# Half blocks of the expert weights ahead of chunks 1 to 5 of a round instead of 2 to 7, and a gain buffer of two rows instead of four

## The reference

```
qh = hb @ w_q                          # 8 heads, two halves each
v1, i1 = top_k(qh1 @ keys1, 16);  v2, i2 = top_k(qh2 @ keys2, 16)
best, pos = top_k(v1 + v2, 16)         # of 256 pairs
eidx = i1 * 128 + i2;  gates = softmax(best)
act = gelu(hb . u_tab[eidx])
out = sum over heads and choices of gates * act * v_tab[eidx]
```

## Time and profile before

| | |
|---|---|
| median of 3 runs | 3056.21 us (3046.61 to 3059.09) |
| profiled execution | 3059.14 us, its span 3057.4 us |
| mean granted TensorE clock | 0.941 |
| PE busy | 2788.9 us, 91% |
| PE weight loads busy | 2321.6 us, 76% |
| DVE busy | 1881.6 us, 62% |
| POOL busy | 1296.4 us, 42% |
| ACT busy | 1040.0 us, 34% |
| DMA | 528.80 MB, mean 173 GB/s |

### The profile page before, as it was taken

One profiled execution on the slowest core, in us unless ns is written; L12 is line 12 of the kernel. 1 busy time (PEld: TensorE's weight loads), 2 busy tenths in 40 slices (PEclk: granted clock), 3 DMA queues, 4 the chain that ended last, 5 costly groups with the idle time before them and its releaser, 6 DMA issues. The chain is left out here.

```text
span 3057.4 us, 38838 instructions
## 1 busy us (share of the span) xinstructions
PE 2788.9 (91%) x14085; PEld 2321.6 (76%) x14085; DVE 1881.6 (62%) x3137; ACT 1040.0 (34%) x1640; POOL 1296.4 (42%) x618
## 2 busy tenths in 40 slices
PE   7998996787999998969989899999999959999996
PEld 5887874634777887857878689998999957888885
DVE  5443224376164445348345448777999959888887
ACT  4222221154223222323012223334556524444442
POOL 3443444000433443424124346775222237777773
PEclk9999998589999999989789899999999989999998
DMA  5443322000323443313001235556999989999993
GB/s 173 142 146 110 103 89 103 1 1 17 94 83 131 137 151 120 106 55 111 20 14 36 74 106 163 169 157 230 361 351 345 338 292 350 381 381 379 382 378 138
DMA packets 186247, 528.80 MB, mean 173 GB/s; under 512 B 13984, under 2 KB 96288, under 8 KB 166432
## 3 DMA queue, kind: packets, MB, share of 16 engines
q1 hardware_dynamic: 79776, 292.66, 29.4%
q0 software_dynamic: 18432, 134.23, 11.1%
q10 hardware_dynamic: 87936, 100.68, 9.7%
HBM read 475.08 MB, written 52.43 MB: 173 GB/s over the span
## 5 line engine op out<-in xcount | busy, mean ns | idle before, releaser
L345 POOL TENSOR_TENSOR ring_low<-ring,ring_high 128x1024 fp32r<-128x1024 f32 x323 | 790.5, 2448 | 1172.9 <-ACT ring_high L312 1172.9
L396 PE MATMUL ps<-u_high,ring_high 128*128 128x512 f32 (+1 forms) x1824 | 700.8, 384 | 42.7 <-DVE u_low L617 17.7
L397 PE MATMUL ps<-u_low,ring_high 128*128 128x512 f32 (+1 forms) x1824 | 693.3, 380 | 0.0
L398 PE MATMUL ps<-u_high,ring_low 128*128 128x512 f32 (+1 forms) x1824 | 690.2, 378 | 0.0
L312 ACT ACTIVATE ring_high<-ring 128x1024 fp32r<-128x1024 f32 x355 | 375.2, 1057 | 717.3 <-PE ps L398 538.5
L396 PEld LDWEIGHTS ps<-u_high,ring_high 128*128 128x128 f32 x1824 | 346.8, 190 | 113.2 <-issue 40.7
L398 PEld LDWEIGHTS ps<-u_high,ring_low 128*128 128x128 f32 x1824 | 346.8, 190 | 57.6
L397 PEld LDWEIGHTS ps<-u_low,ring_high 128*128 128x128 f32 x1824 | 347.3, 190 | 52.9 <-issue 1.3
L2303 POOL DMA_INDIRECT fetched_rows<-in_peer_uv,fetch_index x128 | 166.2, 1298 | 310.4 <-DVE ps L2323 271.6
L345 POOL TENSOR_TENSOR ring_low_more<-ring,ring_high_more 128x1024 fp32r<-128x1024 f32 x96 | 245.9, 2565 | 88.4 <-ACT ring_high_more L312 87.4
L2869 DVE TENSOR_TENSOR expert_product<-group_acts,group_weights 128x384 f32<-128x384 f32 x128 | 172.1, 1345 | 70.9 <-issue 44.1
(11 more groups left out here) (429 smaller groups left out, 4834.3 us busy)
## 6 DMA issues: line engine op xcount, KB each, us to landing
ring<-in_peer_u SPq DMA_DIRECT2D x128, 512.0 KB
ring<-in_peer_uv SPq DMA_DIRECT2D x128, 512.0 KB
ring<-in_ffn_gu SPq DMA_DIRECT2D x88, 512.0 KB
ada_weights<-in_ada_w SPq DMA_DIRECT2D x48, 512.0 KB, 3.9
ring<-in_ffn_down SPq DMA_DIRECT2D x48, 512.0 KB
expert_acts<-kept_acts ACTq DMA_DIRECT2D x128, 192.0 KB, 3.9
expert_weights<-weight_stage ACTq DMA_DIRECT2D x24, 1024.0 KB, 8.9
group_acts<-expert_acts ACTq DMA_DIRECT2D x16, 1536.0 KB, 19.0
```

The source lines that it names most:

```text
L345: pool.tensor_tensor(k.lows[p], k.ring[:, s], k.highs[p].bitcast(F32), ALU.subtract)\
L396: pe.matmul(out, k.highs[p][:, w], high, start=first, stop=False)
L397: pe.matmul(out, k.highs[p][:, w], low, start=False, stop=False)
L398: last = pe.matmul(out, k.lows[p][:, w], high, start=False, stop=final)
```

## The change

`halves_at` now places half block q ahead of chunk max(1, q). Half blocks 0 and 1 both stand ahead of chunk 1, and half blocks 2, 3, 4 and 5 ahead of chunks 2, 3, 4 and 5. Before, 0 to 5 stood ahead of chunks 2 to 7. PE's hook and ACT's `take` both read the list, so both move; DVE's order has no part of it. The product of L1880 is written over row 0, the mixer reads row 0, and the buffer has two rows.

```diff
@@ -1877,7 +1877,7 @@
-            step(dve.tensor_tensor(k.gain[:, 2], k.gain[:, 0], k.vec("norm_final"), ALU.mult))
+            step(dve.tensor_tensor(k.gain[:, 0], k.gain[:, 0], k.vec("norm_final"), ALU.mult))
@@ -2216,7 +2216,7 @@
-            shifted = ShiftedNorm(k, inner, k.gain[:, 2], k.mod[:, 0:KD], k.vec("norm_final"))
+            shifted = ShiftedNorm(k, inner, k.gain[:, 0], k.mod[:, 0:KD], k.vec("norm_final"))
@@ -2655,7 +2655,7 @@
         def halves_at(e):
-            return [q for q in range(HALVES) if max(1, 8 - HALVES + q) == e]
+            return [q for q in range(HALVES) if max(1, q) == e]
@@ -2966,7 +2966,7 @@
-        k.gain = k.sbuf("gain", [P, 4, KD])
+        k.gain = k.sbuf("gain", [P, 2, KD])
```

## The result

The changed kernel takes 3342.9 us (median of 4 executions, 3333.7 to 3356.2) where the kernel before takes 3057.7 us in the same comparison. The ratio is 1.0926, with an interval of 1.0882 to 1.0971. That is 285 us, 9.3% slower; 3389 us was forecast, in a range of 3285 to 3440.

What follows compares the result with a forecast made beforehand. PE and DVE were taken to run abreast. Profiled execution 3059.1 + 235.4 (chain) + 100 (clock) - 2.3 (end of stage) = 3392.2, lowered by 2.9 to the median of the runs: 3389 us, range 3285 to 3440.

Steps and rivals of the forecast that it cites:

- The order as the mechanism: PE waits at half blocks 1 to 5 for DVE tables made behind a low part that needs chunk q-1 finished.
- the chain: End of chunk q-1, low part, half block on DVE, its matmuls, chunk q: 11.76 us, PE idle 5.98 (q 2 to 5).
- The chain's sum: Round of the half-block stage 73.6 us against 44.17: 29.4 us more, 235 us over 8 rounds.
- The clock: In the half-block stage the granted clock falls behind 40 PE pauses, 2.5 us lost at each: 100 us more.
- Rival 1: Work between the stage's pauses keeps 2.4 GHz, or loses little: 3289 us, chance 0.12.
- rival 2: The clock never comes back in the half-block stage: about 3620 us, chance 0.08.
- rivals 3 and 4: 3: DVE's tables ready ahead of need, 3031 us, chance 0.02; 4: DVE's work still bounds, within 0.5% of 3056, chance 0.02.
- ACT's gate behind the half block: In the turn of chunk q-1, ACT waits for half block q before gating row q-2: costs nothing, covered by the stall.
- The end of the stage: The last store of weights leaves three chunks earlier, so the next stage's first load comes 2.3 us sooner.
- The gain buffer: Two rows, product written in place, tiles behind it 64 bytes lower: no time, with 5 us either way.

Runs made afterwards that it cites:

- Chunk of cover (one earlier): The changed kernel, but half blocks 0 to 5 ahead of chunks 1 to 6, one chunk earlier than in the kernel before: 3065.43 us, ratio 1.0049.
- DVE's order (tables first): The changed kernel, but DVE makes the tables of half block q+1 before the low part of chunk q+4: 3179.15 us, ratio 1.0411.
- the pauses filled: The changed kernel, plus 32 PE matmuls ahead of its wait for the tables of half blocks 1 to 5: 3262.08 us, ratio 1.0681.

## Why the prediction was right, and where it was not

*The order as the mechanism: right.* PE's pauses came at the five places named: by the idle time of PE's own rows 5.8 to 6.0 us ahead of chunks 2 to 5, against 5.98, and 5.0 ahead of half block 1, where 6.7 was forecast. A sixth was missed: the fence below has half block 0 waiting 1.64 us, where it was taken to be ready. Its tables also come behind a low part, that of chunk 3. This changed no sum, for the two pauses together are the one of the forecast: 1.64 + 4.97 = 6.61 us for 6.7. By the chain the waits of eight rounds are 8 x (6.7 + 4 x 5.98) = 245 us; the trace has 241.4. Chunk of cover (one earlier) and DVE's order (tables first) both move the cost as the chain says.

```profile
2265.89 1.51 PE L2672 MATMUL ps<-gated_i,hot_i 128*128 128x128 bf16 x24 [1.64 <-DVE gated_i L2745]
2272.37 2.74 PE L2672 MATMUL ps<-gated_i,hot_i 128*128 128x128 bf16 x24 [4.97 <-DVE gated_i L2745]
```

*The chain's sum: right.* 73.6 us a round was forecast without the clock, 73.0 was measured with the pauses filled: 231 us over 8 rounds for the 235 of the sum.

*The clock: right in kind, its size too large.* 100 us were put down, 2.5 us for each pause; it measured 71, 1.8 a pause. Behind the pause of 6.00 us, 3.9 us of work ran at 1.2 GHz; behind the six pauses of the earlier trace rows the loss of 1.5 to 3.1 us stands for 3.0 to 6.2 us of such work. The row nearest in length (6.72 us, 1.5 us lost) would have given 62, nearer than the mean. But the trace gives no reason to go by length, as two more of those six pauses show:

```profile
893.28 0.79 PE L396 MATMUL ps<-merged_high,ring_high 128*128 128x512 f32 x1 [3.96 <-PEq L1445]
...
1199.68 0.79 PE L396 MATMUL ps<-ffn_hid_high,ring_high 128*128 128x512 f32 x1 [9.03 <-PEq L739]
```

The pause of 3.96 us cost 3.0 us, the one of 9.03 us 1.8. What sets the loss behind one pause stays open here, so that 62 lies closer may be chance. The sentence of the Trainium skill (TensorE: Matmul & The Clock Gate, Part 1) that puts a ramp under 1% of a span is no bound for a kernel that pauses 40 times: the runs here have 71 us, 2.1% of 3348. That agrees with the same part's section on oscillation, by which such a kernel pays again at every pause.

Rival 1 falls with the clock of 0.81, rival 2 with the clock back at 1.00 from chunk 6 to half block 0, rivals 3 and 4 with the 241 us of waits. Rival 2's sum counts five half blocks a round where there are six: PE's path is 8 x 4.16 + 6 x 1.62 = 43.0 us, and the rival's time 3056.2 + 235.4 + 8 x 43.0 - 2.3 = 3633 us instead of 3620, which changes nothing for it.

*ACT's gate behind the half block: right.* It was costed at nothing with the stall as its cover, and taking it away changed nothing.

*The end of the stage: right in sign, too small.*

```profile
2738.35 1.95 ACT L2704 ACTIVATE weight_stage<-ps 128x1024 f32<-128x1024 f32 x1 [7.28 <-PE ps L2672]
...
2751.64 0.49 ACT L2556 ACTIVATE kept_acts<-ps 128x384 f32<-128x384 f32 x1 [2.74 <-PE ps L398]
2752.16 0.33 ACTq L2562 DMA_DIRECT2D expert_acts<-kept_acts  x1
2754.69 0.39 ACTq L2829 DMA_DIRECT2D group_acts<-expert_acts  x1
```

From the last gelu to the first load of the next stage it is 3.05 us, and was 7.22: 4.2 us less, where 2.3 were forecast. The term that was too large is the landing of the last store of activations: 3.9 us, the median of 128, were put down, and the load goes out 2.53 us behind that store's issue.

*The gain buffer: the step that failed.* "No row shows an address costing time; nothing, with 5 us either way kept." It was worth 13.6 us. Rows of the trace before do show it: the fence from `combine` above has two chunks at 233.6 ns a matmul beside two at 226.9, with the same engine, clock and shape. They do not say what 64 bytes less would bring, but they were a reason for a wider bound and a rival of its own, as the edit moves nearly every tile by 64 bytes.

Together: 3055.0 + 231 + 71 - 4.2 - 13.6 = 3339 us, against 3342.9. The forecast of 3389 was 46 too high: 29 for the clock, 14 for the buffer, 4 for the chain and 2 for the end, 49 by these terms.

## What to carry to other kernels

When work is moved forward in one engine's queue, ask what its producer does just before it: if the producer's queue holds a step there that needs the consumer's last result, the cover is gone all at once. Here the first chunk given up cost 4 us a round, the second 34 more. The reverse is cheap to try: putting the producer's independent work ahead of the dependent step took back 164 us here, and made the old order 10 us faster. And when an edit changes the size of an early buffer, compare the number of matmuls in a fixed stretch before crediting or blaming the rest of the edit.

## What the runs showed of the hardware

The pace of matmuls at full clock hung on the distance in a partition between the two tiles that a matmul reads, its weights and its moving tile. In the first ffn it was 226.7 ns for 512 columns at 0 modulo 256 bytes, 228.9 at 64 and 233.3 at 128, whatever the absolute address. In `combine`, where the weights lie behind the moving tile, the same shift by 64 bytes took it from 227 to 233 ns, so the 228.9 is no rule for every pair 64 bytes off. Other distances, and why it is so, were not tried. PE is busy 200 of 200 us in all five of the kernels compared in the first ffn.

Behind PE's pauses of 5.0 to 6.0 us the half block ran at 1.2 GHz in every round: from the first to the last start of its 24 matmuls it took 2.3 to 2.4 us, 40 times out of 40. Behind the eight pauses of 1.6 us it took 1.3 us, as it did 48 times out of 48 with the pauses filled. The chunks without a pause ran at 2.4 GHz. The rounds of each of three kernels with these pauses lie between 81.9 and 82.1 us, although one had its gate moved and another a different pace elsewhere.
